# Expert weights of a two-layer encoder: down weights requested ahead of the next quad's gate-up, and the output weights of both layers in units

## The chip, the cores and the metric

The kernel runs on one core of one Trainium2 chip. The metric is the time of one execution on the device in microseconds (us), lower is better.

## What is computed

A trunk of two layers over 256 frames of width 1024, all in float32. Cut to what matters:

```python
for layer in range(2):
    h = rms_norm(x, mix_norm[layer])
    mix = even_layer_mixer(h, ...) if layer == 0 else odd_layer_mixer(h, ...)   # input projection, two mixers, @ w_out
    x = x + mix
    h = rms_norm(x, moe_norm[layer])
    x = x + hierarchical_moe(h, ...)

def hierarchical_moe(h, ...):      # top-1 group of 4, then top-2 of its 8 experts
    ...                            # gate: (tokens, 4, 8), zero but for the chosen experts
    for grp in range(4):
        hid = silu(einsum('td,edf->tef', t, w_gate[grp])) * einsum('td,edf->tef', t, w_up[grp])
        out = out + einsum('tef,efd->td', hid * gate[:, grp, :, None], w_down[grp])
```

There are 32 experts in each layer, each with a gate, an up and a down matrix of 1024 x 128, 512 KB apiece.

## The kernel before

**Input and output projection.** The input weights come in chunks (8 in layer 0, 10 in layer 1) of up to 1.5 MB into the four slots of the tile RAW. ScalarE and VectorE split each quarter of a chunk, a unit, into a high and a low part (WH by L697, WL by L713 or L716; six unit buffers), and PE multiplies with both (L720 to L722, L756 to L758). Semaphore "unit_hi" counts the first half of the split, "unit_lo" the second, "unit_used" the products. A slot is free for the next transfer when its chunk's last unit has counted on "unit_lo". The output weights are three chunks of the widths 384, 384 and 256, so 12 units. In layer 0 they are transferred as chunks, into slots 1, 2 and 3. In layer 1 they are transferred unit by unit, through a ring of four places in slot 2; unit n goes out when unit n - 4 is split.

**Mixers.** In layer 0 the memory of slot 0 is used by the mixers once its last chunk is split; "b_O" counts the last matrix products of mixer B (L2544 and the lines around it), the last readers of it. In layer 1 slot 1 is used so, until "c_R" 2. "c_O" counts the four groups of outputs of mixer C. "m_sq" counts the squares of the second norm (ScalarE, L1062), six a layer, written into a scratch tile JK; "m_lg" the router's logits.

**Experts.** Experts are worked off in quads of four, on 32-column groups of the array. ORDER is 0, 1, 2, the spill (an extra expert matrix for one overfull expert, SPW), 3 to 7. For quad q the gate-up product (L2289, 64 instructions) gives the hidden rows; VectorE and ScalarE make the activation; the down product is L2339 (16 instructions), and L2361, L2362 add it to the tokens' sum. The loop on PE at place t runs: transpose of the hidden rows, combine(t-1), gate_up(t+1), down(t), and after quads 0, the spill and 4 the gathering of the next group's tokens (L2242, L2248).

**Places.** Gate-up weights lie in a ring of 11 places, each for one expert: four in RAW (the first 2 of 3 parts of each slot), four in XG, then XTRB, XTRA, XTRC, the ninth, tenth and eleventh. XG and XD lie where WH and WL are. Down weights of even quads lie in the last part of RAW's slots, of odd quads in XD. The tile XTRC lies inside the memory of the mixers, as do XTRB and XTRA (which shares its place with the router's input HTF and, before, with JK).

**Requests.** All weights are requested by SP in the order of its program; a wait holds back everything behind it. For the experts: first quad 0 and 1 piece by piece into what comes free (into_slot, chunk_free, ring_free, into_units, down_into_units), then extra_in (quad 2's gate-up into XTRC and XTRB after all squares, into XTRA after the logits), the spill, and then for q = 2 to 7 gate_up_in(q), which waits until quad q - 2's gate-up product is done and requests experts 4q + 3 to 4q + 6, two loads each, and, from q = 3, down_in(q - 1), which waits until quad q - 3's down product is done. last_down_in requests quad 7's down weights in two halves of columns.

Of the kernel before, what the change touches and what calls it, by code (L numbers as in the profile page):

```python
# [24 lines left out]
P = 128  # L25
T = 256
# [90 lines left out]
def program(nc, x, mix_norm, moe_norm, ev_w_in, ev_w_out, a_q_gain, a_k_gain, a_sinks, b_lb_logits,  # L117
# [4 lines left out]
    with ctx:  # L122
# [130 lines left out]
        JK = at("JK", [P, NT, D], m.at)  # L253
        XTRB = m.take("XTRB", [P, 2 * D])
        GT = m.take("GT", [P, KT, T + SPILL])
        XTRC = m.take("XTRC", [P, 2 * D])
# [3 lines left out]
        PTRS = m.take("PTRS", [P, T], F32R)  # L260
        YL = m.take("YL", [P, D], F32R)
# [113 lines left out]
        landed_value = [16 * sum(slot_at(e) == slot_at(i) for e in range(i + 1)) for i in range(len(plan))]  # L375

        UNIT_SLOT = 2
        UNIT_RING = 4

        def ring_no(i, j):

            return unit_no[i, j] - unit_no[slot_of[1, "out", OUT_UNITS[1][0][0]], OUT_UNITS[1][0][1]]

        def in_ring(i):
            return plan[i][:2] == (1, "out")

        def unit_landed(n):

            chunks = sum(slot_at(e) == n % UNIT_RING for e in range(slot_of[1, "out", 0]))  # L390
            return 16 * (chunks + n // UNIT_RING + 1)
# [53 lines left out]
        def _(sp):  # L445
# [41 lines left out]
            def unit_in(n):  # L487

                c, j = OUT_UNITS[1][n]
                _, c0, w = OUT_CHUNKS[c]  # L490
                if n >= UNIT_RING:
                    cc, jj = OUT_UNITS[1][n - UNIT_RING]
                    sp.wait_ge(sem("unit_lo"), unit_no[slot_of[1, "out", cc], jj] + 1)
                o = 768 * (n % UNIT_RING)
                sp.dma_start(RAW[:, UNIT_SLOT, o:o + 2 * w].rearrange("p (k n) -> p k n", k=2),
                             w_out[1][0, 2 * j * P:2 * (j + 1) * P, c0:c0 + w].rearrange("(k p) n -> p k n", p=P)
                             ).then_inc(sem(f"landed{n % UNIT_RING}"), 16)

            def first_units_in():

                last_in = len(CHUNKS[1]) - 1
                sp.wait_ge(sem("unit_lo"), slot_units[slot_of[1, "in", last_in - 3]])
                for c in range(last_in - 3, last_in + 1):
                    i = slot_of[1, "in", c]
                    sp.wait_ge(sem(f"landed{slot_at(i)}"), landed_value[i])
                for n in range(UNIT_RING):
                    unit_in(n)

            def experts_in(l):
# [42 lines left out]
                def into_slot(j, m):  # L552

                    i = max(i for i in range(units_through[l] // 4) if slot_at(i) == j)
                    if plan[i][:2] == (l, "out"):
                        w = OUT_CHUNKS[plan[i][2]][2]
                        inside = [jj for jj in range(4) if 2 * jj * w < (m + 1) * D and 2 * (jj + 1) * w > m * D]
                        sp.wait_ge(sem("unit_lo"), max((unit_no[i, jj] + 1 for jj in inside), default=slot_units[before(i)]))
                    elif l == 0:
                        sp.wait_ge(sem("b_O"), 2)  # L560
                    else:
                        sp.wait_ge(sem("c_R"), 2)
                    load("gu_in" if m < 2 else "dn_in", 0, j, m)

                def chunk_free(c, j, ms=range(3)):
                    sp.wait_ge(sem("unit_lo"), slot_units[slot_of[1, "in", c]])
                    for m in ms:
                        load("gu_in" if m < 2 else "dn_in", 0, j, m)

                def ring_free(n, m):  # L570
                    c, j = OUT_UNITS[1][n]
                    sp.wait_ge(sem("unit_lo"), unit_no[slot_of[1, "out", c], j] + 1)
                    load("gu_in" if m < 2 else "dn_in", 0, UNIT_SLOT, m)

# [77 lines left out]
            for l in range(layers):  # L652
                chunks_in(l, "in")
                if l == 0:
                    chunks_in(l, "out")
                else:
                    first_units_in()
# [2198 lines left out]
```

## Time and profile before

| | us |
|---|---|
| median of 3 runs | 557.69 |
| lowest, highest | 553.71, 557.84 |
| the profiled execution, its own time | 560.13 |
| its span | 558.3 |
| PE busy in it | 511.4 (92%) |
| VectorE, ScalarE, GpSimd busy | 284.7, 246.4, 82.5 |
| moved by the DMA | 143.88 MB, mean 258 GB/s |

Times in the profile count from the start of the span. The 40 slices of the page are 13.96 us each. PE busy counts time in which a product is under way, so it tells little about its pace. The input projection and the mixers of layer 0 take the span up to about 102, the output projection goes to 126, the router and the experts to 246; layer 1 has its input projection and mixers up to 401, its output projection to 432, and its experts to the end.

### The profile page before, as it was taken

To read this page: it belongs to the slowest core of one execution; us is meant where nothing else is said; L and a number is where in the kernel's file an instruction comes from. 1 tells how busy PE (TensorE), PEld (TensorE's weight loads), DVE (VectorE), ACT (ScalarE), POOL (GpSimd) and SP (SyncE) were. 2 spreads that over 40 slices of the span, in tenths; PEclk is the share of its full clock that TensorE was granted. 3 is DMA by queue.
4 is the path that set the end of the run, shared out by engine and by line. 5 is a ranking of instruction groups with operands and counts; after the bars stand their busy time and mean duration, and the time that the engine had idled before them with its cause. 6 is when DMAs were issued, how large, how long until landed. Compare 5 with 4: busy or idle time off the path is not lost.

```text
span 558.3 us, 11283 instructions
## 1 busy us (share of the span) xinstructions
PE 511.4 (92%) x4756; PEld 422.4 (76%) x4756; DVE 284.7 (51%) x536; ACT 246.4 (44%) x479; POOL 82.5 (15%) x101
## 2 busy tenths in 40 slices
PE   5999999999897988999999999999989889499985
PEld 5999999997663646549999999799988657155642
DVE  2669988756311211147899535687647721121113
ACT  5667578664342323146554734322437524123311
POOL 5814821100000000012000750011110000000000
PEclk9999999997998997999999999899999999789999
DMA  9992233679999999989554333000436999999992
GB/s 315 298 358 81 83 144 115 224 263 413 394 406 409 409 408 409 350 295 314 162 181 156 113 114 114 1 4 2 155 111 204 407 409 408 409 409 409 408 362 81
DMA packets 56996, 143.88 MB, mean 258 GB/s; under 512 B 4612, under 2 KB 29408, under 8 KB 56816
## 3 DMA queue, kind: packets, MB, share of 16 engines
q1 hardware_dynamic: 55792, 141.68, 67.9%
q0 software_dynamic: 976, 1.38, 1.0%
q8 instruction: 39, 0.64, 0.5%
q10 hardware_dynamic: 176, 0.07, 0.1%
q14 instruction: 13, 0.11, 0.1%
HBM read 142.07 MB, written 1.05 MB: 256 GB/s over the span
## 4 chain that ended last, share of the span: by engine, by line
PE 61%; DMA 13%; DVE 11%; ACT 6%; SPq 6%; issue 2%; ACTq 0%; DVEq 0%
DMA RAW<-moe_w_down 8%; PE PS L2289 7%; PE PS L720 6%; PE PS L722 6%; PE PS L721 6%; SPq L516 4%; PE PS L2248 3%; PE PS L756 3%; PE PS L757 3%; PE PS L758 3%; PE PS L2339 3%; DMA XD<-moe_w_down 3%; SPq L518 3%; DVE SL L1447 2%; PE PS L2456 2%
## 5 line engine op out<-in xcount | busy, mean ns | idle before, releaser
L720 PE MATMUL PS<-WH,HTH 128*128 128x384 f32 (+2 forms) x272 | 90.7, 333 | 4.1 <-DVE WL L716 2.1
L716 DVE TENSOR_TENSOR WL<-RAW,WH 128x768 fp32r<-128x768 f32 (+2 forms) x84 | 77.2, 955 | 23.3 <-ACT WH L697 23.0
L722 PE MATMUL PS<-WH,HTL 128*128 128x384 f32 (+2 forms) x272 | 87.6, 322 | 0.0
L721 PE MATMUL PS<-WL,HTH 128*128 128x384 f32 (+2 forms) x272 | 87.5, 322 | 0.0
L697 ACT ACTIVATE WH<-RAW 128x768 fp32r<-128x768 f32 (+2 forms) x84 | 63.1, 798 | 3.5 <-PE PS L722 2.1
L1447 DVE SCALAR_TENSOR_TENSOR HID<-SIL,MW,PS 128x128 f32<-128x128 f32 x18 | 6.3, 347 | 108.8 <-ACT SIL L1117 108.8
L720 PEld LDWEIGHTS PS<-WH,HTH 128*128 128x128 f32 x272 | 51.3, 189 | 5.6 <-issue 2.9
L721 PEld LDWEIGHTS PS<-WL,HTH 128*128 128x128 f32 x272 | 51.4, 189 | 0.0
L722 PEld LDWEIGHTS PS<-WH,HTL 128*128 128x128 f32 x272 | 51.3, 188 | 0.0
L1439 DVE TENSOR_TENSOR YL<-PS,YH 128x512 fp32r<-128x512 f32 (+1 forms) x34 | 23.5, 691 | 48.2 <-ACT YH L1133 40.8
L756 PE MATMUL PS<-HTH,WH 128*128 128x256 f32 x160 | 45.9, 287 | 0.4 <-DVE HTL L1447 0.4
L757 PE MATMUL PS<-HTL,WH 128*128 128x256 f32 x160 | 45.2, 283 | 0.0
L758 PE MATMUL PS<-HTH,WL 128*128 128x256 f32 x160 | 45.2, 283 | 0.0
L1117 ACT ACTIVATE SIL<-PS,MW 128x128 f32<-128x128 f32 x18 | 6.6, 368 | 74.3 <-PE PS L2289 63.8
L2289 PE MATMUL PS<-RAW,GT 128*32 128x256 f32 x384 | 36.8, 384 | 1.9 <-ACT GT L1098 1.9
L1133 ACT ACTIVATE YH<-PS 128x512 fp32r<-128x512 f32 x32 | 19.1, 597 | 41.6 <-PE PS L2339 41.6
L2289 PE MATMUL PS<-XG,GT 128*32 128x256 f32 x384 | 36.9, 382 | 0.0
L2339 PE MATMUL PS<-RAW,HIDT 128*32 128x512 f32 x128 | 18.9, 718 | 13.8 <-DMA RAW<-moe_w_down 13.8
L756 PEld LDWEIGHTS PS<-HTH,WH 128*128 128x128 f32 x160 | 30.6, 191 | 0.8 <-DVE HTL L1447 0.8
L2361 PE MATMUL PS<-YH,PTR 128*128 128x512 f32 x64 | 26.5, 413 | 5.2 <-DVE YL L1439 4.9
L757 PEld LDWEIGHTS PS<-HTL,WH 128*128 128x128 f32 x160 | 30.7, 192 | 0.0
L758 PEld LDWEIGHTS PS<-HTH,WL 128*128 128x128 f32 x160 | 30.7, 192 | 0.0
(374 smaller groups left out, 1085.6 us busy)
## 6 DMA issues: line engine op xcount, KB each, us to landing
RAW<-moe_w_down SPq DMA_DIRECT2D x32, 512.0 KB, 13.4
RAW<-od_w_in SPq DMA_DIRECT2D x9, 1536.0 KB, 7.1
RAW<-moe_w_gate SPq DMA_DIRECT2D x24, 512.0 KB, 7.2
RAW<-moe_w_up SPq DMA_DIRECT2D x24, 512.0 KB, 9.2
XD<-moe_w_down SPq DMA_DIRECT2D x24, 512.0 KB, 12.8
XG<-moe_w_gate SPq DMA_DIRECT2D x24, 512.0 KB, 10.6
XG<-moe_w_up SPq DMA_DIRECT2D x24, 512.0 KB, 12.2
RAW<-ev_w_in SPq DMA_DIRECT2D x5, 1536.0 KB, 14.1
```

The source lines that it names most:

```text
L697: done(nc.scalar.activation(hi, raw, ACT.Copy, scale=1.0 if gain is None else gain), "unit_hi")
L716: done(nc.vector.tensor_tensor(out=lo, in0=raw, in1=hi.bitcast(F32), op=ALU.subtract), "unit_lo")
L720: nc.tensor.matmul(ps, ah, bh, start=start, stop=False)
L721: nc.tensor.matmul(ps, ah, bl, start=False, stop=False)
L722: return nc.tensor.matmul(ps, al, bh, start=False, stop=stop)
L756: nc.tensor.matmul(PS[:, bank, 0:T], wh[:, kk, cs], HTH[:, k, :], start=k == first, stop=False)
L757: nc.tensor.matmul(PS[:, bank, 0:T], wh[:, kk, cs], HTL[:, k, :], start=False, stop=False)
L758: last = nc.tensor.matmul(PS[:, bank, 0:T], wl[:, kk, cs], HTH[:, k, :], start=False, stop=k == final)
L1439: return nc.vector.tensor_tensor(out=out, in0=a, in1=b, op=op)
L2289: last = mm(PS[s, 0, T * (t % 2):T * (t % 2) + T], GT[:, k, o + s.start:o + s.stop], w, start=k == 0, stop=k == KT - 1)
L2339: done(mm(PS[s, 2 + b, :], HIDT[:, t % 2, s], down_raw(q, j)[:, 512 * b:512 * b + 512], start=True, stop=True), "dn")
L2361: mm(bank, at_, YH[:, 512 * b:512 * b + 512], start=t == 0, stop=False)
```

## The change

It has three parts.

1. In the loop of experts_in the down weights of quad q are requested right behind gate_up_in(q), for q = 2 to 6, ahead of gate_up_in(q + 1). Before, down_in(q - 1) stood behind gate_up_in(q), from q = 3.
2. The output weights of layer 0 are transferred unit by unit too, through a ring of four places in slot 1. The ring's functions take the layer as an argument. Slots 2 and 3 take quad 0's third and fourth expert as soon as input chunks 6 and 7 are split, and slot 0 its first expert after "b_O" 2; the second expert goes into the ring's slot after units 9, 10 and 11.
3. XTRC is moved to memory that the mixers release earlier (behind layer 1's SL), JK to the memory of H, written in strips of the pattern that HL has there. The four gate-up loads of quad 2 into XTRC and XTRB no longer wait for "m_sq": in layer 0 they go out behind slot 0's, after "b_O" 2, ahead of units 8 to 11, and in layer 1 after "c_O" 4, ahead of units 9 to 11. XTRA's stay behind "m_lg".

```diff
-        JK = at("JK", [P, NT, D], m.at)
+        JK = at("JK", [P, NT, D], hh)
         XTRB = m.take("XTRB", [P, 2 * D])
         GT = m.take("GT", [P, KT, T + SPILL])
-        XTRC = m.take("XTRC", [P, 2 * D])
...
+        m.at = max(m.at, mix + (NT * 2064 + 12 * (T + 4) + 12 * T) * 4)
+        XTRC = m.take("XTRC", [P, 2 * D])
...
-        UNIT_SLOT = 2
+        UNIT_SLOT = (1, 2)
         UNIT_RING = 4
...
-            def first_units_in():
-
-                last_in = len(CHUNKS[1]) - 1
-                sp.wait_ge(sem("unit_lo"), slot_units[slot_of[1, "in", last_in - 3]])
+            def first_units_in(l):
+
+                last_in = len(CHUNKS[l]) - 1
                 for c in range(last_in - 3, last_in + 1):
-                    i = slot_of[1, "in", c]
+                    i = slot_of[l, "in", c]
+                    if slot_at(i) == UNIT_SLOT[l]:
+                        sp.wait_ge(sem("unit_lo"), slot_units[i])
+                for c in range(last_in - 3, last_in + 1):
+                    i = slot_of[l, "in", c]
                     sp.wait_ge(sem(f"landed{slot_at(i)}"), landed_value[i])
                 for n in range(UNIT_RING):
-                    unit_in(n)
+                    unit_in(l, n)
...
-                def extra_in():
-
-                    sp.wait_ge(sem("m_sq"), 6 * (l + 1))
-                    for j in (2, 0):
-                        for m in range(2):
-                            load("gu_in", 2, j, m)
-                    sp.wait_ge(sem("m_lg"), l + 1)
+                def extra_in(j):
+
                     for m in range(2):
-                        load("gu_in", 2, 1, m)
+                        load("gu_in", 2, j, m)
...
                 if l == 0:
-                    into_slot(3, 2)
-                    into_slot(1, 0)
-                    into_slot(2, 0)
-                    into_slot(0, 0)
-                    into_slot(0, 1)
-                    into_slot(0, 2)
-                    into_slot(3, 0)
-                    into_slot(1, 1)
-                    into_slot(1, 2)
+                    chunk_free(6, 2)
+                    chunk_free(7, 3)
+                    for n in range(4, 8):
+                        unit_in(l, n)
+                    into_slot(0, "b_O", 2)
+                    extra_in(2)
+                    extra_in(0)
+                    for n in range(8, 12):
+                        unit_in(l, n)
                     down_into_units(0)
-                    into_slot(2, 1)
                     down_into_units(1)
                     into_units(1)
-                    into_slot(2, 2)
+                    ring_free(9, 0)
+                    ring_free(10, 1)
+                    ring_free(11, 2)
                     down_into_units(2)
-                    into_slot(3, 1)
                     down_into_units(3)
                     into_units(2)
                     into_units(0)
...
                     chunk_free(7, 3)
                     chunk_free(8, 0)
-                    unit_in(4)
-                    unit_in(5)
-                    into_slot(1, 0)
-                    into_slot(1, 1)
-                    into_slot(1, 2)
-                    for n in range(6, 12):
-                        unit_in(n)
+                    unit_in(l, 4)
+                    unit_in(l, 5)
+                    into_slot(1, "c_R", 2)
+                    unit_in(l, 6)
+                    unit_in(l, 7)
+                    unit_in(l, 8)
+                    sp.wait_ge(sem("c_O"), 4)
+                    extra_in(2)
+                    extra_in(0)
+                    for n in range(9, 12):
+                        unit_in(l, n)
                     ring_free(9, 0)
...
-                extra_in()
+                sp.wait_ge(sem("m_lg"), l + 1)
+                extra_in(1)
                 spill_in(l)
                 for q in range(2, QUADS):
                     gate_up_in(q)
-                    if q > 2:
-                        down_in(q - 1)
+                    if q < QUADS - 1:
+                        down_in(q)
                 last_down_in()
...
-                        done(nc.scalar.activation(JK[:, i, c0:c0 + w], X[:, i, c0:c0 + w], ACT.Square, scale=1.0 / 32,
+                        done(nc.scalar.activation(JK[:, i, :].rearrange("p (k q) -> p k q", k=KT)[:, :, c0 // KT:(c0 + w) // KT],
+                                                  X[:, i, c0:c0 + w].rearrange("p (k q) -> p k q", k=KT), ACT.Square, scale=1.0 / 32,
                                                   accum_out=MSC[:, 3 * i + c:3 * i + c + 1]), "m_sq")
```

## Rows read from the trace of the kernel before

**Rows 1.** The page's 40 slices: GB/s that the DMA moved in each.

```profile
GB/s 315 298 358 81 83 144 115 224 263 413 394 406 409 409 408 409 350 295 314 162 181 156 113 114 114 1 4 2 155 111 204 407 409 408 409 409 409 408 362 81
```

**Rows 2.** Waits: for RAW (total us, times, longest); L518's weights (total, times).

```profile
PE PS L2339 <- DMA RAW<-moe_w_down: 13.8, 3, 7.9
...
  PE PS L2339: 15.2, 4
```

**Rows 3.** The chain that ended last, in order: start us, us, what.

```profile
112.27 0.87 PE PS L2138 x8
122.94 0.66 PE PS L2197 x6
...
178.76 3.25 PE PS L2339 x16
...
211.03 2.54 PE PS L2339 x16
...
233.50 3.59 PE PS L2289 x64
...
471.18 15.91 DMA RAW<-moe_w_down
487.34 3.64 PE PS L2339 x16
...
517.81 15.29 DMA XD<-moe_w_down
...
539.90 3.59 PE PS L2289 x64
```

**Rows 4.** Timeline of PE: start us, us, group, idle before and releaser.

```profile
154.48 1.90 PE L2339 MATMUL PS<-RAW,HIDT 128*32 128x512 f32 x16
...
178.76 1.93 PE L2339 MATMUL PS<-RAW,HIDT 128*32 128x512 f32 x8 [3.30 <-DMA RAW<-moe_w_down]
```

**Rows 5.** Timeline of SP's requests: start us, us, group.

```profile
102.93 0.43 SPq L516 DMA_DIRECT2D RAW<-moe_w_up  x1
...
159.30 5.18 SPq L518 DMA_DIRECT2D RAW<-moe_w_down  x4
...
414.54 1.30 SPq L495 DMA_DIRECT2D RAW<-od_w_out  x2
```

**Rows 6.** Single requests (last fields: start of first and last), each with its landing times.

```profile
L516 SPq DMA_DIRECT2D RAW<-moe_w_gate x1: 328/328/328, 335.7 to 335.7; - x1
DMA to landing us min/median/max: 3.5/3.5/3.5
...
L516 SPq DMA_DIRECT2D RAW<-moe_w_gate x1: 338/338/338, 148.5 to 148.5; - x1
DMA to landing us min/median/max: 4.3/4.3/4.3
...
L516 SPq DMA_DIRECT2D RAW<-moe_w_gate x1: 338/338/338, 452.8 to 452.8; - x1
DMA to landing us min/median/max: 7.7/7.7/7.7
...
L518 SPq DMA_DIRECT2D RAW<-moe_w_down x2: 1079/1080/1082, 217.2 to 218.3; - x2
DMA to landing us min/median/max: 13.0/14.2/15.4
...
L518 SPq DMA_DIRECT2D RAW<-moe_w_down x2: 1068/2024/2981, 522.8 to 525.8; - x2
DMA to landing us min/median/max: 14.6/14.8/15.0
```

**Rows 7.** Timeline of ScalarE: the split of units 8 to 11, layer 0.

```profile
113.94 2.98 ACT L697 ACTIVATE WH<-RAW,PT 128x768 fp32r<-128x768 f32 x4
```

**Rows 8.** Windows: us; PE, PEld, DVE, ACT, POOL busy (instructions); granted clock, DMA share, GB/s.

```profile
128.00:136.00 8.00, 8.00 (x37) 5.94 (x37) 3.67 (x15) 2.09 (x6) 0.89 (x2) 0.64 1.03 413
484.00:492.00 8.00, 4.66 (x25) 1.26 (x29) 0.97 (x2) 1.36 (x3) 0.00 (x0) 0.50 1.03 410
```

More of the change, by code:

```diff
@@ L372, in chunk_done, with unit_landed @@
             eng.wait_ge(sem("unit_used"), slot_units[slot_of[layer, what, c]])
-        landed_value = [16 * sum(slot_at(e) == slot_at(i) for e in range(i + 1)) for i in range(len(plan))]
-        UNIT_SLOT = 2
+        landed_value = [16 * (3 * plan[i][0] + sum(slot_at(e) == slot_at(i) for e in range(i + 1) if plan[e][1] == "in"))
+                        for i in range(len(plan))]
+        UNIT_SLOT = (1, 2)
         UNIT_RING = 4
         def ring_no(i, j):
-            return unit_no[i, j] - unit_no[slot_of[1, "out", OUT_UNITS[1][0][0]], OUT_UNITS[1][0][1]]
+            l = plan[i][0]
+            return unit_no[i, j] - unit_no[slot_of[l, "out", OUT_UNITS[l][0][0]], OUT_UNITS[l][0][1]]
         def in_ring(i):
[L386 to L391, printed above, removed]
+            return plan[i][1] == "out"
+        def unit_landed(l, n):
+            chunks = sum(slot_at(e) == n % UNIT_RING for e in range(slot_of[l, "out", 0]) if plan[e][1] == "in")
+            return 16 * (chunks + 3 * l + n // UNIT_RING + 1)
         GU_RING = 11
@@ L485, in chunks_in, with unit_in @@
                     sp.dma_start(raw, src).then_inc(sem(f"landed{s}"), 16)
-            def unit_in(n):
-                c, j = OUT_UNITS[1][n]
+            def unit_in(l, n):
+                c, j = OUT_UNITS[l][n]
                 _, c0, w = OUT_CHUNKS[c]
                 if n >= UNIT_RING:
-                    cc, jj = OUT_UNITS[1][n - UNIT_RING]
-                    sp.wait_ge(sem("unit_lo"), unit_no[slot_of[1, "out", cc], jj] + 1)
+                    cc, jj = OUT_UNITS[l][n - UNIT_RING]
+                    sp.wait_ge(sem("unit_lo"), unit_no[slot_of[l, "out", cc], jj] + 1)
                 o = 768 * (n % UNIT_RING)
-                sp.dma_start(RAW[:, UNIT_SLOT, o:o + 2 * w].rearrange("p (k n) -> p k n", k=2),
-                             w_out[1][0, 2 * j * P:2 * (j + 1) * P, c0:c0 + w].rearrange("(k p) n -> p k n", p=P)
+                sp.dma_start(RAW[:, UNIT_SLOT[l], o:o + 2 * w].rearrange("p (k n) -> p k n", k=2),
+                             w_out[l][0, 2 * j * P:2 * (j + 1) * P, c0:c0 + w].rearrange("(k p) n -> p k n", p=P)
                              ).then_inc(sem(f"landed{n % UNIT_RING}"), 16)
-            def first_units_in():
-                last_in = len(CHUNKS[1]) - 1
-                sp.wait_ge(sem("unit_lo"), slot_units[slot_of[1, "in", last_in - 3]])
+            def first_units_in(l):
+                last_in = len(CHUNKS[l]) - 1
                 for c in range(last_in - 3, last_in + 1):
-                    i = slot_of[1, "in", c]
+                    i = slot_of[l, "in", c]
[3 more added lines that the diff above has]
+                    i = slot_of[l, "in", c]
                     sp.wait_ge(sem(f"landed{slot_at(i)}"), landed_value[i])
                 for n in range(UNIT_RING):
-                    unit_in(n)
+                    unit_in(l, n)
             def experts_in(l):
@@ L550, in down_in, with into_slot, chunk_free @@
                         load("dn_in", q, j, 2)
[L552 to L567, printed above, removed]
+                def into_slot(j, ready, n):
+                    sp.wait_ge(sem(ready), n)
+                    for m in range(3):
                         load("gu_in" if m < 2 else "dn_in", 0, j, m)
+                def chunk_free(c, j):
+                    into_slot(j, "unit_lo", slot_units[slot_of[l, "in", c]])
                 def ring_free(n, m):
-                    c, j = OUT_UNITS[1][n]
-                    sp.wait_ge(sem("unit_lo"), unit_no[slot_of[1, "out", c], j] + 1)
-                    load("gu_in" if m < 2 else "dn_in", 0, UNIT_SLOT, m)
+                    c, j = OUT_UNITS[l][n]
+                    sp.wait_ge(sem("unit_lo"), unit_no[slot_of[l, "out", c], j] + 1)
+                    load("gu_in" if m < 2 else "dn_in", 0, UNIT_SLOT[l], m)
                 def unit_free(r):
@@ L653, in _ @@
                 chunks_in(l, "in")
[L654 to L657, printed above, removed]
+                first_units_in(l)
                 if stop > 2 * l + 1:
@@ L679, in unit_views @@
                 o = 768 * (ring_no(i, j) % UNIT_RING)
-                return RAW[:, UNIT_SLOT, o:o + 2 * w], WH[:, u, 0:2 * w], WL[:, u, 0:2 * w]
+                return RAW[:, UNIT_SLOT[layer], o:o + 2 * w], WH[:, u, 0:2 * w], WL[:, u, 0:2 * w]
             return RAW[:, s, 2 * j * w:2 * (j + 1) * w], WH[:, u, 0:2 * w], WL[:, u, 0:2 * w]
@@ L687, in split_hi @@
             elif in_ring(i):
-                act.wait_ge(sem(f"landed{ring_no(i, j) % UNIT_RING}"), unit_landed(ring_no(i, j)))
+                act.wait_ge(sem(f"landed{ring_no(i, j) % UNIT_RING}"), unit_landed(plan[i][0], ring_no(i, j)))
             elif u == 1 or i and u == min(unit_no[i, jj] for jj in range(4)):
```

## The prediction

> **What bounds the kernel now.** I read the page's slices first. The 26th to 28th of the 40 slices move almost nothing (1 to 4 GB/s), but the 10th to 16th and the 32nd to 38th stand near 409 GB/s [rows 1]: those are the expert stages of layers 0 and 1, and there the weight transfers run at their limit. A load of one expert matrix (512 KB, 524,288 bytes) takes 524288/409000 = 1.28 us of it. A layer's experts are 32 x 3 such loads and 3 more for the spill expert, 99.
>
> Next who waits for the down weights. PE's products at L2339 stand still for them four times, 15.2 us in all; three of the stops, 13.8 us with a longest of 7.9, are for down weights in RAW [rows 2]. In the chain of waits the longest ends at 487.34 (quad 2 of layer 1, landing at 471.18 + 15.91 = 487.09), a later one is for quad 5 (landing at 517.81 + 15.29 = 533.10) [rows 3]; quad 2 of layer 0 has 3.3 us, until 178.76 [rows 4], and quad 4 of layer 0 the rest, 15.2 - 7.9 - 3.3 - 1.4 (the other in layer 1, 15.2 - 13.8) = 2.6. The reader is to see that a PE that is 92% busy on the page hides them.
>
> Then the queue. The down weights of quad 2 are requested at 159.30 in layer 0, behind the eight gate-up loads of the next request [rows 5], and down weights take over 15 us to land in such a stretch [rows 3]; with an empty queue a load lands in 3.5 us [rows 6]. So the request is late, not the transfer slow. But the queue never runs dry after that: between the two landings in layer 1, 487.09 and 533.10, lie 36 loads in 46.0 us, 1.28 each. What orders loads differently in such a stretch takes from one load what it gives to another.
>
> **How much can be ahead.** The places for gate-up weights are 11, for down weights 8, and the spill's one: 11 x 2 + 8 + 3 = 33 loads. The 34th waits for quad 0's gate-up product. That request goes out at 148.5 in layer 0 and at 452.8 in layer 1. Its first load lands after 4.3 us in layer 0, after 7.7 in layer 1, where 3.5 is what an empty queue gives [rows 6]. So the queue was already almost drained in layer 0 (0.8 us of older work) and 4.2 us behind in layer 1. I number the loads from that request, 66 in each layer. This is the part that decides.
>
> **Part one, places free early.** In both layers four loads (quad 2's first and third gate-up places) move from after the router's squares into the time of the output projection. In layer 0 the output weights now pass through a ring of four units in one slot, so three slots rather than none take experts early: 13 loads are asked for by about 106 us, where before 9 had gone out by 111. What is brought forward is 4 loads x 1.28 = 5.1 us of transfer time, out of time when the queue idled. In layer 0 only 0.8 us of it can be used, because loads 1 to 66 begin with a request that PE gives at 148.5 as before. In layer 1 4.2 us can be used. Head starts: 0.8 and 4.2 us.
>
> Its costs. Layer 0's unit 8 is now requested behind seven expert loads, which wait for the last recurrence output (at about 102.5; slot 0's second and third load went out behind it from 102.93 [rows 5]). Seven loads take 9.0 us: 102.5 + 2.9 (3.5 of latency less the 0.6 which is not service) + 9.0 = 114.4, and the unit itself (384 KB, 0.96 us) makes 115.4. ScalarE splits it at 113.94 now, four units in 2.98 us [rows 7], so 1.5 us later. PE takes units 5 to 9 between the end of the transposes, 112.27 + 0.87 = 113.1, and 122.9 [rows 3], 2.0 us each, so it wants unit 8 at 119.0; the split's two halves take 1.8 us, ready at 117.2. 1.8 us to spare, cost nothing; without that cover a late unit is paid one for one. In layer 1 four loads (5.1 us) go ahead of units 9 to 11, after unit 8's request at 414.54 [rows 5]: unit 9 comes at about 414.5 + 2.6 + 5.1 + 1.3 = 423.5, some 5 us later than now; but its product is the third last of the projection, behind those of units 6 to 8, and units 10 and 11 can be asked for only once units 6 and 7 are split, as before. I take nothing again, and up to 5 us for it belongs to rival (d). The waits added, "b_O" 2 and "c_O" 4, are for outputs that the output projection itself needs, so PE is past them when it starts; behind them in SP's queue stand only units whose ring places come free later or at the same time. The added unit requests (12 against 3 chunk requests, some 0.4 us each on SP) lie in an idle SP. The squares written in strips (six instructions a layer) have as many elements; I take 0. The price is bounded by zero and by what as many elements cost in a split, 2.98 / 4 = 0.7 us each [rows 7], 4 us a layer at the utmost, most of it beside PE's products.
>
> **Part two, the order.** Before: gate-up request 2 (8 loads), request 3 (8), down 2 (4), request 4, down 3, and so on, request 7 (2 loads, expert 31), down 6, down 7. After: request 2, down 2, request 3, down 3, ... down 6, request 7, down 7. Ends of the requests by number: down 2 moves from 20 to 12, down 4 from 44 to 36, down 5 from 56 to 48. Each is 8 x 1.28 = 10.3 us earlier, more than the largest gap (7.9): all four stops at L2339 go. But expert 23 moves from 34 to 38, expert 27 from 46 to 50 and expert 31 from 58 to 62, each 5.1 us later; quad 5, 6 and 7's gate-ups wait for them. PE now arrives early there. In layer 0 quad 5's gate-up starts now at 211.03 - 2.6 - 3.66 = 204.8 [rows 3]; without quad 2's stop and its slow clock (3.3 + 1.35) it would at 200.1, and expert 23 lands at 152.8 - 0.8 + 37 x 1.28 + 1 to 3 = 200 to 202: a stop of 0 to 2 us. Quad 6 may wait as long again. At quad 7 PE has gained the stops and their clock less that and the wait is 4 to 5 us: from quad 4's down product to quad 7's gate-up it needs 233.5 - 211.0 = 22.5 us, some of it at a slow clock, so it would be there by about 228.
>
> The end follows from number 62. Before, 62 is the last load of down 6: it lands at 218.3 + 15.4 = 233.7 and 525.8 + 15.0 = 540.8 [rows 6]. Less the head starts, expert 31 lands at 232.9 and 536.6. Quad 7's gate-up starts now at 233.5 and 539.9 [rows 3], since expert 31 was number 58, 5.1 us earlier, and there in time. So the last gate-up comes 0.6 and 3.3 us earlier, and everything behind it on PE follows unchanged. The last down weights, numbers 63 to 66, come 4 x 1.28 = 5.1 us behind, at 238.0 and 541.7, before PE wants them (8 us behind quad 7's start).
>
> Sum: layer 0 -0.6 + 1.7 = +1.1; layer 1 -3.3 + 1.7 = -1.6; together -0.5. The profiled execution took 560.13 (span 558.3), so 559.6; the median of the runs, 557.69, is 2.4 lower: 557.2.
>
> The Trainium skill (DMA: Bandwidth & Descriptors, HWDGE ordering) says that requests of one queue start in ring order on each engine but need not complete in order. The even 1.28 us per load agrees with a queue in order; if completion strayed, the last gate-up could come some us later.
>
> **The rivals.**
> (a) The wait moves to the last gate-ups, as above: 557.2, half of the chance (0.50).
> (b) Faster: either the four stops vanish and nothing takes their place, 3.3 + 2.6 + 7.9 + 1.4 + 1.35 + 1.74 = 18.3 us, 539.4. Against it speaks that the transfers are saturated to the end: 0.05. Or the clock stays full and layer 0 has a head start like layer 1's (its request at 148.5 came late since the clock was at 0.64 in 128 to 136, in the router [rows 8], 8 x 0.36 = 2.9 us): -3.9 - 2.9 = -6.8, so 550.9: 0.15.
> (c) The head start is not had, since units and early loads meet and the backlog stays: layer 0 +0.2 + 1.7, layer 1 +0.9 + 1.7, so +4.5: 562.2: 0.18. That is the change not doing what it says.
> (d) Slower, the unit behind seven loads: it decides when unit 8 lands after 117.1 instead of 115.4. Landings in a full queue trail the service by up to 3 us (number 62 in layer 0 was there at 233.7, where 152.8 + 61 x 1.28 = 230.9), so it could be 118.4, and units 9 to 11 behind it. With a stop of the output projection of 3 us and half clock for as long: +6, so 563.2: 0.12.
>
> **The numbers.** A measurement of this kernel tells 1% (5.6 us) from no change: 552.1 to 563.3. Faster are (b) and a little of (a): 0.21. Slower are most of (d) and the edge of (c): 0.14. The rest, 0.65, is no change. Range: clock free and half a head start more, 551.5; up to (c) and into (d), 562.5. The likeliest case alone runs from 553.8 (no clock loss) to 561.2 (3.7 in each).
>
> **What would show it.** No DMA wait at L2339 for quads 2 to 5; waits of L2289 on expert 23, 27 and 31, the last of 4 to 5 us in each layer with a granted clock under 1 behind it; the first load after quad 0's gate-up landing 3.5 us after its request in both layers; a gap in the transfers just before it in layer 0; the down loads of quad 2 requested 3 us earlier and landing in 10 us. Wrong if the last gate-up starts well before 232 (layer 0), if PE idles at L720 in the output projection, or if the stops at L2339 stay.

## The result

| | us |
|---|---|
| before, median of 15 runs | 556.24 (553.41 to 561.33) |
| changed, median of 15 runs | 561.08 (559.32 to 565.16) |
| ratio changed to before | 1.0078, 95% interval 1.0055 to 1.0102 |
| profiled execution before, after | 560.13, 565.16 |
| its span before, after | 558.3, 563.4 |

The change makes the kernel 0.8% slower, 4 to 5 us. That is less than the 1% that was called "no change", but it is clear of the noise of 15 runs, and it lies on the other side of the forecast of -0.5 us. Both profiled executions lie above their kernel's median: before's by 3.9 us, and the changed kernel's, the longest of its 15 runs, by 4.1. So a difference of one or two us between two profiles need not be in the typical run.

### The profile page after: what moved, and what is told of

It reads as the page before. It is cut to its first block, busy times and chain, and to the rows that moved or that the text cites. A ratio compares the mean times of both kernels' runs of the same rounds, so it can differ in the third digit from the quotient of the medians.

```text
span 563.4 us, 11303 instructions
## 1 busy us (share of the span) xinstructions
PE 515.9 (92%) x4756; PEld 426.7 (76%) x4756; DVE 285.1 (51%) x536; ACT 246.8 (44%) x479; POOL 83.0 (15%) x101
## 4 chain that ended last, share of the span: by engine, by line
PE 74%; DVE 12%; ACT 6%; issue 5%; DMA 2%; SPq 0%; POOL 0%; ACTq 0%; DVEq 0%
PE PS L2284 12%; PE PS L714 6%; PE PS L716 5%; PE PS L715 5%; PE PS L2243 5%; PE PS L2334 4%; PE PS L2356 3%; PE PS L750 3%; PE PS L752 3%; PE PS L751 3%; PE PS L2357 2%; DVE SL L1442 2%; PE PS L2451 2%; DVE WL L710 1%; PE PS L2204 1%
## 5 line engine op out<-in xcount | busy, mean ns | idle before, releaser
L2284 PE MATMUL PS<-XG,GT 128*32 128x256 f32 x384 | 45.7, 449 | 9.1 <-issue 9.1
L2284 PE MATMUL PS<-RAW,GT 128*32 128x256 f32 x384 | 38.1, 391 | 5.6 <-issue 3.8
L2284 PEld LDWEIGHTS PS<-XG,GT 128*32 128x32 f32 x384 | 22.1, 128 | 22.2 <-issue 17.5
L2284 PEld LDWEIGHTS PS<-RAW,GT 128*32 128x32 f32 x384 | 19.9, 112 | 14.3 <-issue 5.7
```

What stands on the lines that cost most here:

```text
L2284: last = mm(PS[s, 0, T * (t % 2):T * (t % 2) + T], GT[:, k, o + s.start:o + s.stop], w, start=k == 0, stop=k == KT - 1)
```

## The profile after

L2284 is the gate-up product of before's L2289, L2334 the down product (L2339). The waits of the changed kernel (engine and line, releaser; then us in total, times, longest):

```profile
PE PS L2284 <- issue: 15.3, 6, 5.4
```

No stop at L2334 for down weights is left, where there were four of 15.2 us [rows 2]. In their place stand six at the gate-up, of 15.3 us. The sum is the same to 0.1 us: the stops have moved. Their releaser is given as "issue", that is, nothing that the profile shows, so the landing times of the weights have to be looked up. The chain of waits, in order (start us, us, what):

```profile
202.20 1.52 issue
203.72 3.66 PE PS L2284 x64
...
216.83 2.22 issue
219.05 5.35 PE PS L2284 x64
...
230.72 3.69 issue
234.41 6.57 PE PS L2284 x64
...
250.34 5.36 PE PS L2162 x12
...
510.02 0.93 issue
...
524.73 1.54 issue
...
536.24 5.39 issue
541.63 6.56 PE PS L2284 x64
```

The stops come in threes, ahead of quads 5, 6 and 7, and the last of each layer is the longest. The gate-up behind it takes 6.6 us in both layers; in [rows 3] it took 3.59 in the chain (3.66 by the timeline, which counts from its first product). In layer 0 quad 7 starts 234.41 - 233.50 = 0.9 us later than before and takes 3.0 more, and the layer is left 3.9 us later (250.34; before, the same products began at 246.46). In layer 1 it starts 541.63 - 539.90 = 1.7 later and takes 3.0 more: 4.7 at the end.

Single requests of the changed kernel with their landing times: the first after quad 0's gate-up in each layer, and expert 31's two (last fields: start of the first and last request of the row).

```profile
L522 SPq DMA_DIRECT2D RAW<-moe_w_gate x1: 339/339/339, 148.9 to 148.9; - x1
DMA to landing us min/median/max: 3.6/3.6/3.6
...
L522 SPq DMA_DIRECT2D RAW<-moe_w_gate x1: 339/339/339, 458.6 to 458.6; - x1
DMA to landing us min/median/max: 3.5/3.5/3.5
...
L522 SPq DMA_DIRECT2D XTRA<-moe_w_gate x1: 1077/1077/1077, 217.6 to 217.6; - x1
L522 SPq DMA_DIRECT2D XTRA<-moe_w_up x1: 1074/1074/1074, 218.7 to 218.7; - x1
DMA to landing us min/median/max: 13.8/14.7/15.6
...
L522 SPq DMA_DIRECT2D XTRA<-moe_w_gate x1: 1079/1079/1079, 525.3 to 525.3; - x1
L522 SPq DMA_DIRECT2D XTRA<-moe_w_up x1: 1077/1077/1077, 526.4 to 526.4; - x1
DMA to landing us min/median/max: 14.5/14.8/15.1
```

The queue is empty at that point in both layers now: 3.6 and 3.5 us where it took 4.3 and 7.7 [rows 6]. Expert 31's second load is there at 218.7 + 15.6 = 234.3 and 526.4 + 15.1 = 541.5, each 0.1 us before the gate-up starts. So "issue" was that load.

The clock, from the windows of the changed kernel that hold these two gate-ups (columns as in rows 8):

```profile
234.00:242.00 8.00, 7.59 (x76) 3.92 (x80) 0.35 (x1) 0.37 (x1) 0.00 (x0) 0.60 0.39 144
...
541.00:549.00 8.00, 7.37 (x76) 3.82 (x80) 0.27 (x1) 0.37 (x1) 0.00 (x0) 0.59 0.57 208
```

0.60 and 0.59 over 8 us: about 6.4 us at 1.2 GHz and the rest at 2.4. That is as long as the whole gate-up.

One more stop is new, in the output projection of layer 1: the timeline of ScalarE there (start us, busy us, operation; in brackets idle before and releaser).

```profile
428.25 0.63 ACT L691 ACTIVATE WH<-RAW 128x512 fp32r<-128x512 f32 x1 [3.47 <-DMA RAW<-od_w_out]
```

And that of PE:

```profile
430.60 0.87 PE L2192 MATMUL PS<-CT,X 128*128 128x128 f32 x6 [1.55 <-DVE X L1434]
```

ScalarE waits 3.47 us for unit 9 of the output weights, VectorE's half of the split waits for ScalarE's, and behind it in VectorE's program stands the residual add of the first columns. The transposes for the router on PE need that add, so PE loses 1.55 us.

## The experiments

Ratios are to the kernel before on the same chip in the same session, with their 95% interval. They are not the quotient of the two medians; with the few runs of an experiment (4 to 12) the two can differ by up to 0.4%. Three chips were used (before: 556.16, 558.42 and 556.65 us), so kernels are compared by their ratios, not by their medians.

**The order alone.** The kernel before, with nothing but this:

```diff
                 for q in range(2, QUADS):
                     gate_up_in(q)
-                    if q > 2:
-                        down_in(q - 1)
+                    if q < QUADS - 1:
+                        down_in(q)
```

> The kernel before with the new request order alone (down weights of quad q right behind gate-up request q, from q = 2); places, units and the time of the early loads as before. Theory (the order costs, since expert 31 moves from load 58 to 62 of a saturated queue and the last gate-up, started after a stop, runs at the low clock): layer 0's last gate-up starts at about 233.7 and takes 6.6 us instead of 3.6, layer 1 the same from a queue that is 4 us behind: about 563.5 us, 7 above the median before (1.3%). Rival (the slow part is the early places and units, the order is neutral or a gain since the stops for down weights go): 550 to 556.

Measured: 562.82 us (561.43 to 567.07), ratio 1.0159 (1.0114 to 1.0204). Its waits:

```profile
PE PS L2289 <- issue: 17.7, 4, 5.4
```

Its chain:

```profile
226.46 5.38 issue
231.84 5.75 PE PS L2289 x64
...
534.60 5.32 issue
539.91 5.31 PE PS L2289 x64
```

The order costs 1.6% by itself (1.2% by the medians, with four runs), as the arithmetic of load 62 said, with stops of 5.4 and 5.3 us ahead of the last gate-ups. These take 5.75 and 5.31 us, not the 6.6 expected. The rival is out.

**The places and units alone.** The changed kernel with the old order (the same edit, reversed).

> The changed kernel with the old request order: places free early, units in both layers, unit 9 of layer 1 behind the four early loads. Theory (the order costs, the places gain a little): the stop for quad 2's down weights in layer 1 shrinks from 7.9 to about 4 us, 1.5 us go again in the output projection of layer 1, the last gate-ups find their weights there and run at full clock (3.6 us): about 554 us, 2 below before. Rival (the places cost): 558 to 562, no better than the changed kernel.

Measured: 554.33 us (553.04 to 557.28), ratio 0.9994 (0.9969 to 1.002). By the medians it is 1.8 us below before, by the ratio equal to it; the 2 us expected would be 0.9964, just outside the interval. So the places are not what makes the changed kernel slow, and with the old order they bring little or nothing. With the new order they bring 0.8% by the ratios (1.0159 without them, 1.0078 with them). Its waits for down weights fell, in all (total us, times):

```profile
  PE PS L2334: 8.7, 5
```

from 15.2, 4 [rows 2]. Both last gate-ups take 3.66 us, as expected; the stop for quad 2's down weights in layer 1 fell further than expected, to 0.97 us. Between the profiled executions the 6.5 us less of waiting are there (553.04 against 560.13), but before's lay 3.9 us above its median and this one 1.3 below its own.

**The last request only.** The changed kernel, with expert 31 ahead of quad 6's down weights again:

```diff
                 for q in range(2, QUADS):
-                    gate_up_in(q)
-                    if q < QUADS - 1:
-                        down_in(q)
+                    if q == QUADS - 1:
+                        gate_up_in(q)
+                        down_in(q - 1)
+                    else:
+                        gate_up_in(q)
+                        if q < QUADS - 2:
+                            down_in(q)
```

> The changed kernel with one exchange: the last gate-up request (expert 31, two loads) goes ahead of quad 6's down weights again, so it is load 58 and not 62. Theory: expert 31 lands 5.1 us earlier, at 229.3 in layer 0 where PE is ready at 230.7, and at about 536.5 less the shift in layer 1 where PE is ready at 536.2; both last gate-ups take 3.66 instead of 6.57 us. Saved 3.7 + 2.9 in layer 0 and about 5 + 2.9 in layer 1, less up to 2 us where the last down weights now set the end: about 549 us, 1.3% below before. Rival (the wait is not for expert 31's place in the queue but for something that moves with it, such as the last down weights): 559 to 561.

Measured: 550.12 us (545.95 to 553.24), ratio 0.9891 (0.984 to 0.9942): 1.1% below before and, by the ratios, 1.9% or 10 us below the changed kernel. Four loads and two have changed places in each layer, nothing else. The waits (gate-up L2288 and down L2338 here):

```profile
PE PS L2288 <- issue: 6.7, 6, 2.2
```

The timeline of PE at the last gate-up and at quad 6's down product of layer 0:

```profile
226.23 0.41 PE L2288 MATMUL PS<-XG,GT 128*32 128x256 f32 x2 [0.26 <-issue]
...
231.51 1.92 PE L2338 MATMUL PS<-RAW,HIDT 128*32 128x512 f32 x16 [1.61 <-DMA RAW<-moe_w_down]
```

The stop ahead of quad 7 is 0.26 us and the gate-up lasts until 229.89, 3.66 us. Quad 6's down weights, now loads 59 to 62, are late by 1.61 us; that is what the exchange costs, and the product behind it takes 1.92 us, as at full clock.

**The clock.** The changed kernel, with more filler products of PE (their results are never used) between the last combine and the last gate-up, 12 where there were 4:

```diff
-                        for _ in range(4):
+                        for _ in range(12):
                             mm(PS[:, 0, o:o + T], ident, CT[:, C_DEC:C_DEC + T], start=True, stop=True)
```

> The changed kernel with 12 instead of 4 filler products (results unused) ahead of the last gate-up of each layer, 3.8 us more of PE activity within the wait. Theory (the gate-up's 6.57 us are the low clock after the stop): the wait seen falls from 3.7 and 5.4 us to about 0 and 1.6, the gate-ups take 3.66, 2.9 us saved in each layer: about 555.3 us. Rival (the gate-up is slow because of what it reads or of the transfers beside it, and the clock row is a by-product): no gain, 561.

Measured: 556.54 us (554.22 to 559.52), ratio 1.0016 (0.9987 to 1.0045). Against the changed kernel's 1.0078 that is 0.6%, 3.4 us, for eight products in each layer that compute nothing; 5.8 us were expected. Its waits:

```profile
PE PS L2284 <- issue: 9.5, 6, 2.2
```

Its chain:

```profile
228.80 1.91 issue
...
533.93 1.92 issue
535.85 3.66 PE PS L2284 x64
```

The windows that hold the two last gate-ups:

```profile
230.00:238.00 8.00, 6.76 (x86) 4.15 (x87) 1.73 (x3) 1.73 (x4) 0.00 (x0) 1.00 0.64 211
...
535.00:543.00 8.00, 6.62 (x85) 4.01 (x86) 1.73 (x3) 1.73 (x4) 0.00 (x0) 1.00 0.53 197
```

The idle time before the last gate-up is 1.9 us in both layers, the granted clock is 1.00 and the gate-up takes 3.66 us, while the same loads run beside it. So its 6.6 us were the clock, and the rival is out. The 12 fillers take 5.34 us where the four took 1.89.

**Unit 9 ahead of the early loads.** On top of the kernel with the last request exchanged, in layer 1:

```diff
                     unit_in(l, 8)
+                    unit_in(l, 9)
                     sp.wait_ge(sem("c_O"), 4)
                     extra_in(2)
                     extra_in(0)
-                    for n in range(9, 12):
+                    for n in range(10, 12):
```

> The kernel with the last gate-up request ahead of quad 6's down weights, and besides in layer 1 the request of unit 9 ahead of the four early loads instead of behind them. Theory (the stop of PE in layer 1's output projection, 1.55 us in the changed kernel, and the 0.4 us after it come from unit 9 landing 7.5 us after its request): the stop goes, the early loads go out less than 1 us later and still use an idle queue: 1.5 to 2 us below the kernel without this edit (550.1), so about 548.3. Rival (the stop has another source, the add of VectorE or the ring places): 550.

Measured: 550.42 us (547.6 to 552.98), ratio 0.9852 (0.9809 to 0.9895). By the ratio better than the kernel it starts from (0.9891), but the intervals overlap. The trace says that the expectation was half right. The timeline of ScalarE in that stretch:

```profile
422.79 1.39 ACT L696 ACTIVATE WH<-RAW,PT 128x512 fp32r<-128x512 f32 x2 [4.89 <-DMA RAW<-od_w_out]
```

And that of PE:

```profile
430.34 0.63 PE L2197 MATMUL PS<-CT,X 128*128 128x128 f32 x4 [1.65 <-ACT HTF L1053]
```

Unit 9 is in time and the stop of 1.55 us is gone, but now unit 10 stands in the queue behind the four loads. ScalarE waits 4.89 us for it, its work for the router comes later, and PE stops 1.65 us for that. The wait was only handed on.

**The order of need.** On top of that kernel, each gate-up request from request 4 on is split, its first expert ahead of the previous quad's down weights and the rest behind them. The loop, against the changed kernel (cut: gate_up_in takes the slice of its experts as a second argument):

```diff
-                for q in range(2, QUADS):
-                    gate_up_in(q)
+                gate_up_in(2)
+                down_in(2)
+                gate_up_in(3)
+                for q in range(4, QUADS):
+                    gate_up_in(q, slice(0, 1))
+                    down_in(q - 1)
                     if q < QUADS - 1:
-                        down_in(q)
+                        gate_up_in(q, slice(1, 4))
```

> As the last one, but every request is split so that loads stand in the order in which PE wants them: first expert of gate-up request q (q from 4), down weights of quad q - 1, the rest of request q. Experts 23, 27 and 31 are loads 34, 46 and 58. Theory (six stops of 15.3 us in all became what the queue's rate allows; nothing is gained by order once the queue is saturated, and a stop that is saved at quads 5 and 6 is paid at quad 7, where it brings the low clock): no stops at quads 5 and 6, one of about 4 us ahead of the last gate-up in layer 0 with 1 to 3 us of slow clock: 548 to 551, not below the version without the split. Rival (the order of need is best at each point, and the saved stops of 1.5 to 2 us each are kept): 543 to 545.

Measured: 549.58 us (547.83 to 551.68), ratio 0.9858 (0.9818 to 0.9899), no different from the kernel without the split. Its waits:

```profile
PE PS L2289 <- issue: 7.0, 2, 3.6
```

Its chain in layer 1:

```profile
521.94 3.55 issue
525.50 5.35 PE PS L2289 x64
```

Two stops at the gate-up are left, one in each layer, of 3.5 us and ahead of quad 7, and the gate-up behind takes 5.0 us in layer 0 and 5.35 in layer 1 instead of 3.66. What the better order saved at quads 5 and 6 is waited for at quad 7 and costs a slow clock besides.

**The split order with 12 fillers.** The last kernel with the fillers' edit.

> The fully split order with 12 instead of 4 filler products ahead of the last gate-up of each layer. Theory (the split's gain is lost to the low clock after one long stop): the last gate-ups take 3.66 us, and the end is set by the last down weights, load 66: 1.5 to 3 us below the split order without the fillers, about 547. Rival (the split order has no long stop ahead of quad 7): no difference, or later by the fillers' own time.

Measured: 549.01 us (546.09 to 551.58), ratio 0.9831 (0.9784 to 0.9879). The last gate-ups take 3.66 us as expected, but the step from 0.9858 is within the intervals; whether the fillers still gain there is open. The last stop for a transfer is now 1.6 us, at quad 6's down product in both layers, so the end is set by load 62; load 66 was expected to set it.

**The order without the places.** The kernel before with the new order but for the last request.

> The kernel before with the new request order but for the last gate-up request, which stays ahead of quad 6's down weights; places and units as before. Theory (order and early places are separate gains): the early places are worth their head start in layer 1, 4.2 us, and 0.8 in layer 0, less the 1.9 us that unit 9 costs: this kernel is 3 us above the one with places (550.1), so about 553. Rival (the places are worth nothing, as the comparison with the old order suggests, where they made no difference): 550.

Measured: 553.67 us (548.94 to 555.41), ratio 0.9913 (0.9884 to 0.9943). So the order of requests alone, with six loads of each layer left where they were, turns 1.6% of loss into 0.9% of gain. Against the same order with places and units (0.9891, and 0.9852 with unit 9) the places are worth 0.2 to 0.6%, 1 to 3 us; the intervals overlap in both comparisons, so neither separates that from nothing.

**The early loads in the idle time.** On top of the kernel with unit 9 ahead, in layer 1:

```diff
                     unit_in(l, 7)
-                    unit_in(l, 8)
-                    unit_in(l, 9)
                     sp.wait_ge(sem("c_O"), 4)
                     extra_in(2)
                     extra_in(0)
-                    for n in range(10, 12):
+                    for n in range(8, 12):
```

> As the kernel with unit 9 ahead of the four early loads, but the loads (and their wait on mixer C's fourth output) stand ahead of unit 8's request too, right behind unit 7's. Theory (the early loads cost because they are in the queue when units 9 to 11 are asked for; mixer C's outputs are there 5 us before unit 8's place is, and the queue is idle then): the four loads go out 5 us earlier and have landed before units 8 to 11 are requested, the 4.9 us wait of ScalarE for an output unit falls to the 1.9 us of the kernel before, PE's 1.65 us stop behind it goes: 1.5 us below that kernel (which stood at 0.985 of before), so 0.982. Rival (the units are late for another reason): 0.985.

Measured: 547.88 us (545.46 to 549.89), ratio 0.9825 (0.9787 to 0.9862). What ScalarE waited for:

```profile
ACT WH L694 <- DMA RAW<-od_w_out: 2.5, 2, 1.9
```

The longest wait for an output unit of layer 1 is 1.9 us, as it was before the change, and from 406 on PE's longest stop in that projection is 0.57 us; that for the router's input is 0.34 us. The four loads went out at 403.7 to 405.5, units 8 to 11 from 408.9 on. The gain of 0.3% over the kernel it starts from is the size expected, within the noise of the two.

**All together.** This with the split order and the fillers.

> The same place for the four early loads, with the fully split order and the 12 filler products. The two edits act in different stretches, so their gains should add: 1.5 us below the split order with fillers, which stood at 0.983 of before: 0.980. Rival (the end of each layer is set by load 66, and what comes earlier is waited for there): 0.983.

Measured: 546.74 us (545.3 to 552.18), ratio 0.9822 (0.9773 to 0.9871), the lowest median of the study, and equal in ratio to the kernel without split and fillers. That speaks for the rival, but for another load than it names. The timeline of PE, the down product of quad 6 in layer 1:

```profile
530.42 1.92 PE L2337 MATMUL PS<-RAW,HIDT 128*32 128x512 f32 x16 [1.61 <-DMA RAW<-moe_w_down]
```

PE waits for quad 6's down weights, which end with load 62; for quad 7's, which end with load 66, it does not wait. The kernel without the split has the same stop (1.65 and 1.63 us in its layers, 1.48 and 1.61 here). A better order in front of load 62 is waited for at load 62.

## Why the prediction was off, point by point

**What bounds the kernel: right.** Saturated queue, 33 loads ahead, 66 behind a request that PE gives. The first of the 66 lands 3.5 us after its request in both layers, as the head starts of 0.8 and 4.2 us had it. From the end of quad 0's gate-up to the start of quad 7's, layer 1 took 539.90 - 452.6 = 87.3 us before and 541.63 - (454.81 + 3.66) = 83.2 after, 4.1 us less. That this is so near the head start is in part luck: the landing of load 62 came 5.1 us earlier after the request (540.8 - 452.8 = 88.0 before, 541.5 - 458.6 = 82.9 after), 4.2 of it head start, but before the change nothing waited for load 62, and quad 7 had started 0.9 us ahead of it.

**The four stops go, three others come: right.** Expert 23, 27 and 31, with 1.5, 2.2 and 3.7 us in layer 0 and 0.9, 1.5 and 5.4 in layer 1, where 0 to 2, 0 to 2 and 4 to 5 were written. The order alone, and the exchange of the last request, showed that the last of them decides.

**"Then the clock ... I take 1.7": the main term that was mis-sized.** It was 3.0 in each layer, 2.6 us more in all. The figure was taken from what 16 down products lost (1.35 and 1.74 us). But behind the 7.9 us stop the clock stayed low when these were through. Before's chain and window there:

```profile
491.38 3.95 PE PS L2289 x64
...
490.00:492.00 2.00, 2.00 (x17) 0.58 (x13) 0.97 (x2) 0.81 (x3) 0.00 (x0) 0.50 1.03 410
```

So that stop's price went on into the gate-up behind them, and the down products could not show all of it; behind the 3.3 us stop the next gate-up took 3.66 us again, and they did. The last gate-up is 3.66 us of work in one piece, and all of it ran low. The upper bound of 3.7 stood in the text and was nearer. The kernel with fillers confirms that the clock is the cause. It does not confirm the size: in the kernels with the order alone, with the split, and with the order but without the places, gate-ups behind stops of 3.5 to 5.4 us lost 1.3 to 2.1 us, which is what 1.7 stands for, and 3.0 was measured in one execution of the changed kernel, the longest of its 15. The Trainium skill (TensorE: Matmul & The Clock Gate, Part 1) says that an array left idle gets half of its pulses until it has been busy again; the trace agrees, with 6.6 us behind the long stop and 3.66 where products fill it. Quad 1's gate-up, in the next point but one, ran low with no long stop before it.

**"Nothing again" for unit 9 in layer 1: wrong.** The late landing was foreseen (423.5 on before's time; it came at 420.74 + 7.49 = 428.2, which is 424.3 less the 3.9 us that layer 0 had lost). What was not followed is the queue of the engine behind it: VectorE's residual add stands behind unit 9's split, and the router waits for the add. PE's product of unit 9 was looked at, not the next instruction of VectorE. It cost 2.0 us up to quad 0's gate-up (454.81 - 448.96 = 5.85, less 3.9), 1.55 of them in the stop shown. In layer 0 the same step held: unit 8 landed at 106.32 + 9.97 = 116.3, 0.9 us later than worked out, ScalarE waited 1.77 us for it, and PE did not stop.

**Load 62 in layer 0: 1.5 us later than worked out.** Quad 7 started at 234.41 and not at 232.9. Load 1 went out 0.3 us later than before, and the landing of load 62 trailed the even rate by 234.3 - (148.9 + 3.6 + 61 x 1.28) = 3.7 us, where before it had trailed by 2.8. The timelines show a gap that the forecast lacks. Quad 1's gate-up on PE, SP's requests behind it, and the windows after these, all in the changed kernel:

```profile
151.33 5.35 PE L2284 MATMUL PS<-XG,GT 128*32 128x256 f32 x64
...
158.53 1.75 SPq L524 DMA_DIRECT2D RAW<-moe_w_down  x4
160.33 0.44 SPq L522 DMA_DIRECT2D XG<-moe_w_gate  x1
...
160.00:162.00 2.00, 1.94 (x13) 1.70 (x14) 0.63 (x6) 1.00 (x2) 0.00 (x0) 1.00 0.88 260
162.00:164.00 2.00, 1.94 (x13) 1.50 (x12) 0.00 (x0) 1.47 (x3) 0.00 (x0) 1.00 0.91 324
```

In the old order loads 9 to 16 wait for quad 1's gate-up, and they went out from 154.80. In the new order down 2 stands ahead of them and brings its own wait, for quad 0's down product. That product ended 2.0 us later than before (156.49 + 1.90 = 158.4), since quad 1's gate-up ran 5.35 us instead of 3.66. So load 9 went out 9.7 us after load 1 (6.3 before), when the eight loads in front of it, 10.2 us of transfer, were nearly through. Over the next four us the rate fell to 260 and 324 GB/s, which is 0.47 MB or 1.1 us short of 409. The prediction counted the loads and took "the queue never runs dry after that" from before over to the new order; it did not follow the waits that stand between the requests there.

Other kernels bear this out (times in us; the last column is what goes beyond 61 x 1.28):

| kernel, layer | quad 1's gate-up | load 9 after load 1 | landing of load 1 to that of load 62 | beyond |
|---|---|---|---|---|
| changed, 0 | 5.35 | 9.7 | 81.8 | 3.7 |
| changed, 1 | 3.66 | 8.0 | 79.4 | 1.3 |
| with 12 fillers, 0 | 3.66 | 8.0 | 79.6 | 1.5 |
| with 12 fillers, 1 | 5.35 | 9.7 | 81.3 | 3.2 |
| places, old order, 1 | 5.35 | 8.0 | 79.6 | 1.5 |

With 12 fillers the two layers have changed roles, and the gap goes along. The windows of that kernel in the same stretch of layer 0 and, behind the slow gate-up, of layer 1:

```profile
160.00:162.00 2.00, 1.93 (x15) 1.71 (x14) 0.00 (x0) 1.26 (x4) 0.00 (x0) 1.00 1.03 408
...
464.00:466.00 2.00, 1.89 (x13) 1.42 (x11) 0.00 (x0) 1.58 (x4) 0.00 (x0) 1.00 0.87 252
```

The gap is measured; that the late load 9 makes it is argued from these rows and was not tested by an edit of its own. It is not the only kind: the five kernels that build on unit 9's edit have a gap in layer 1 just behind load 1 (two us at 250 to 309 GB/s), without a late load 9. And with the order alone, whose queue had 0.8 us of older work in it, load 9 at 9.7 us left load 62 only 1.3 us behind the even rate. Why the clock fell in quad 1's gate-up is open. Single landings also stray from the order of the requests: before, the load requested at 459.4 landed 14.9 us later, at 474.3, and the next one, requested at 459.9, at 473.2. The Trainium skill (DMA: Bandwidth & Descriptors, HWDGE ordering) lets requests of one queue complete out of order, and the trace agrees.

**The sum.** Forecast for the profiled execution -0.5, measured +4.7 at the last gate-up's end and +5.1 in the span. The clock gives 2.6 of the difference, load 62 in layer 0 1.5, and layer 1 1.1: the last gate-up there started 2.2 us earlier, if layer 0's loss is taken off, and not 3.3. That 1.1 is unit 9's 2.0 less 0.9, by which load 62 trailed the even rate less than before (1.3 us, 2.2 before). The clock at full was given a chance of its own (0.15), the clock low for the whole gate-up was only the upper edge of (a); the run shows the latter. Rival (d) had the right mechanism, units behind early loads, but its condition and price were for layer 0, where PE did not stop; for unit 9 of layer 1 the text only allowed "up to 5 us". Rival (c) did not occur: the head start was had. That the measured 561.08 lies near (c)'s 562.2 is chance.

**The median.** The forecast went from the profiled execution to 557.69 of three runs. 15 runs put before at 556.24, so the profiled execution of before was itself 3.9 us above the median; part of this, the low clock in the router at 128 to 136, was seen and used only for a rival. From 556.24 the forecast would have been 555.7 and the upper edge of (a) 559.8; the measured 561.08 is above both.

## What to carry to other kernels

In a saturated queue an order is a list of who is to wait: write down the number of each load before and after, and look first at the load that moves back and stands last before the end. A request that moves forward also brings its own wait to everything behind it, so write down what each request waits for, and how much transfer is still ahead in the queue when it goes out. A load that is early must not stand in the queue in front of something small that an engine will ask for while it is under way; put it where the queue is idle and the next small request is still some us off. And a stop costs its own length plus what runs at the low clock behind it: here nine stops of 2.0 to 2.9 us left the gate-up behind them at full clock and each of the eight of 3.5 us or more did not, so several short ones are mostly cheaper than one long one of the same sum.

## What the hardware showed that was not expected

- Nine stops of 2.0 to 2.9 us ahead of a gate-up, over all kernels, left it at full clock (3.66 us; the longest was 2.89 us, in the kernel with the early loads in the idle time). One of 2.22 us did not (219.05: 5.35 us), and behind each of the eight stops of 3.47 us or more it took 5.0 to 6.6 us instead of 3.66.
- The same 3.66 us gate-up took 6.57 and 6.56 us behind stops of 3.7 and 5.4 us, but 5.75 and 5.31 behind 5.4 and 5.3 in the kernel with the order alone. The length of the stop does not fix the loss. What does is not settled here.
- Quad 1's gate-up took 5.35 us instead of 3.66 in 6 of the 24 layers of the twelve kernels (the clock 0.50 in 152 to 154 of the changed kernel), with no stop right ahead of it. The last wait of PE before it was 0.87 us in the changed kernel and 0.88 in layer 0 of before, where it took 3.66. What brought the clock down is not shown.
- Some 3.5 us of products whose result nobody reads (12 took 5.34 us, 4 took 1.89), once in each layer, brought 3.4 us in all by the ratios.
